# Low parts of the plain gate/up tiles on VectorE, two tiles interleaved in every down pass, and four gate blocks moved into the last prompt heads

## The reference, cut to what matters

```
h = rmsnorm(x, g_mix)
qa, ka, va, cq, ckv, kpe, ga, gb = split(h @ w_in)
oa = sliding-window attention with sinks and a relative bias (8 heads)
ob = latent attention: q from cq @ w_uq, keys and values from ckv @ w_ukv (8 heads)
mixed = sigmoid(ga) * (oa @ w_oa) + sigmoid(gb) * (ob @ w_ob)
x = x + mixed @ w_out
h = rmsnorm(x, g_ffn)
x = x + (silu(h @ w_gate) * (h @ w_up)) @ w_down        # D_FF = 2816
```

## Time and profile before

| what | us |
|---|---|
| median of three runs | 1826.62 (1825.90 to 1828.09) |
| the profiled execution | 1825.76 |
| its span, first to last instruction | 1824.0 |
| PE busy | 1771.6 |
| DVE busy | 1046.9 |
| ACT busy | 704.1 |
| POOL busy | 616.0 |

### The profile page before, as it was taken

The page is one execution under the profiler, slowest core; times in us unless marked ns, Lnnn a source line. Parts: engine busy times, 40 slices in busy tenths (PEclk is TensorE's granted clock), DMA queues, the critical chain, the costliest instruction groups (busy, mean ns, idle before and its releaser), DMA issues.

```text
span 1824.0 us, 31441 instructions
## 1 busy us (share of the span) xinstructions
PE 1771.6 (97%) x12122; PEld 1697.2 (93%) x12122; DVE 1046.9 (57%) x1590; ACT 704.1 (39%) x1401; POOL 616.0 (34%) x345
## 2 busy tenths in 40 slices
PE   7999999999999999999999999999999999999997
PEld 7988887999989999999999888789999999999997
DVE  5564455475773745647546444556758555647464
ACT  5254345313432433324432634443234333334243
POOL 1322321133344444534333233112332443534432
PEclk9999999999999999999999999999999999999999
DMA  5233523342123131321222234143321231321212
GB/s 166 87 113 109 145 76 99 129 166 72 66 75 99 59 104 53 104 86 62 68 92 70 76 124 130 64 136 129 137 77 62 78 104 51 104 81 64 98 53 87
DMA packets 63787, 171.24 MB, mean 94 GB/s; under 512 B 8120, under 2 KB 13912, under 8 KB 63512
## 3 DMA queue, kind: packets, MB, share of 16 engines
q1 hardware_dynamic: 62808, 167.73, 28.1%
q10 hardware_dynamic: 864, 1.97, 0.3%
HBM read 151.03 MB, written 19.43 MB: 93 GB/s over the span
## 4 chain that ended last, share of the span: by engine, by line
PE 84%; DVE 7%; ACT 4%; issue 2%; DMA 1%; POOL 1%; SPq 0%; POOLq 0%; DVEq 0%; ACTq 0%
PE acc L1518 36%; PE acc L1359 12%; PE acc L1599 11%; PE psU L1599 9%; PE psS L1599 3%; PE acc L1464 2%; PE psU L1310 1%; PE psU L1324 1%; DMA w_raw<-in_w 1%; PE acc L1289 1%; PE psU L1339 1%; PE acc L1554 1%; ACT w_hi L767 1%; POOL w_lo L703 1%; DVE four L2039 1%
## 5 line engine op out<-in xcount | busy, mean ns | idle before, releaser
L703 POOL TENSOR_TENSOR w_lo<-w_raw,w_hi 128x1024 fp32r<-128x1024 f32 x102 | 248.3, 2435 | 679.7 <-ACT w_hi L767 679.7
L767 ACT ACTIVATE w_hi<-w_raw 128x1024 fp32r<-128x1024 f32 (+2 forms) x194 | 174.0, 898 | 427.0 <-PE acc L1518 386.3
L711 POOL TENSOR_TENSOR w_lo<-w_raw,w_hi 128x512 fp32r<-128x512 f32 (+2 forms) x92 | 143.0, 1555 | 330.4 <-ACT w_hi L767 330.4
L2333 DVE TENSOR_TENSOR xT<-acc,xT 128x640 f32<-128x640 f32 x88 | 72.6, 825 | 199.4 <-PE acc L1518 197.1
L730 POOL TENSOR_TENSOR s_raw<-w_raw 128x512 f32<-128x512 f32 x72 | 106.2, 1475 | 158.5 <-DVE s_lo L1996 110.4
L1518 PE MATMUL acc<-act_hi,w_hi 128*128 128x320 f32 x654 | 149.9, 310 | 4.9 <-DVE act_lo L2045 4.8
L1518 PE MATMUL acc<-act_lo,w_hi 128*128 128x320 f32 x654 | 148.9, 308 | 0.0
L1518 PE MATMUL acc<-act_hi,w_lo 128*128 128x320 f32 x654 | 148.8, 308 | 0.0
L787 ACT ACTIVATE s_hi<-s_raw 128x512 fp32r<-128x512 f32 x144 | 90.2, 627 | 147.7 <-POOL s_raw L730 55.0
L1359 PE MATMUL acc<-h_hi,w_hi 128*128 128x320 f32 x512 | 139.0, 353 | 1.5 <-DVE gate L1976 1.2
L1996 DVE TENSOR_TENSOR s_lo<-s_raw,s_hi 128x512 fp32r<-128x512 f32 x144 | 112.1, 793 | 47.9 <-ACT s_hi L787 47.2
(11 more groups left out here) (347 smaller groups left out, 4695.8 us busy)
## 6 DMA issues: line engine op xcount, KB each, us to landing
w_raw<-in_w SPq DMA_DIRECT2D x116, 512.0 KB, 3.5
w_raw<-in_w_pairs SPq DMA_DIRECT2D x72, 512.0 KB, 3.4
w_raw<-in_w SPq DMA_DIRECT2D x48, 256.0 KB, 2.6
gates<-gate SPq DMA_DIRECT2D x32, 320.0 KB, 2.2
tmp<-gates SPq DMA_DIRECT2D x32, 320.0 KB, 3.2
w_raw<-in_w SPq DMA_DIRECT2D x32, 320.0 KB, 2.7
cb_t<-in_cb_t SPq DMA_DIRECT2D x16, 256.0 KB, 3.0
cb_v<-in_cb_v SPq DMA_DIRECT2D x16, 256.0 KB, 2.8
```

Source lines behind the costliest of these rows:

```text
L703: pool.tensor_tensor(w_lo[:, s, :], w_raw[:, s, :], w_hi[:, s, :], ALU.subtract).then_inc(s_w_lo, 1)
L711: pool.tensor_tensor(w_lo[:, n % 2, 0:cols], w_raw[:, n % 2, 0:cols], w_hi[:, n % 2, 0:cols], ALU.subtract).then_inc(s_w_lo, 1)
L767: act.activation(w_hi[:, slot, 0:cols], w_raw[:, slot, 0:cols], ACT.Copy).then_inc(s_w_hi, 1)
L2333: then(evac, dve.tensor_tensor(two(xT[:, c, :]), acc2(m), two(xT[:, c, :]), ALU.add), alone=g is None and c == KD - 1)
```

## The change

There are three edits. First, POOL no longer makes the low parts of the lead's units 2 to 7; VectorE does, in a new function `lead_weight`, at six places of `lead_pairs`, where `lead_scale`, `lead_up` and `lead_gate` of later tiles also move ahead of some operands' low parts. ScalarE's order is unchanged. Second, every down pass begins with `two_tiles`; in the first four passes one block of tile 1 (`early`) goes ahead of the last block of tile 0. `w_started` of tile 1 then comes with its second block. Third, the first four blocks of the gate tile `GATE_SB`, of which one stood behind the `turn_b` of each of three pairs of heads and one behind the last pair, go into the last two pairs of heads, two in each.

```diff
--- before.py
+++ after.py
@@ -732,8 +732,6 @@
             for l in range(DEPTH):
                 first = 2 if l == 0 else 0
                 lows(l * UNITS + first, UNIT_FF + 2 - first)
-                for n in range(2, 2 * FF_LEAD):
-                    low(l * UNITS + (UNIT_FF + n))
                 for i in range(PAIRS):
                     sums(l, i)
                     turn = turn_of(i) if i < PAIRS - 1 else len(FF_PASSES) - 1
@@ -1402,9 +1400,11 @@
                         if n:
                             gate_blocks(l, g, range(k, k + n))
                         if e == j:
+                            if j >= J_SB - 4:
+                                gate_blocks(l, GATE_SB, [j - J_SB + 4])
                             turn_b(l, j + 1)
-                    if J_SB - 8 <= j < J_SB - 2:
-                        gate_blocks(l, GATE_SB, [(j - J_SB + 8) // 2])
+                    if j >= J_SB - 4:
+                        gate_blocks(l, GATE_SB, [j - J_SB + 5])
                     pv_heads(l, j)
                     if j + 2 < J_SB:
                         turn_b(l, j + 2)
@@ -1528,19 +1528,15 @@
                 seen = l * (D_FF // P) + sum(FF_PASSES[:p + 1])
                 wait_alone(pe, s_act, seen - 1)
                 whole = p < len(FF_PASSES) - 1 or l < DEPTH - 1
-                if p == len(FF_PASSES) - 1:
-                    two_tiles(l, unit, tile_, FF_PASSES[p], seen)
-                    with pe.Fori(0, KD // 2 - (1 if whole else 2)) as i:
-                        pair(l, i, unit + 2, tile_ + 2, act_hi, act_lo, FF_PASSES[p])
-                else:
-                    with pe.Fori(0, KD // 2) as i:
-                        pair(l, i, unit, tile_, act_hi, act_lo, FF_PASSES[p], (s_act, seen))
+                two_tiles(l, unit, tile_, FF_PASSES[p], seen, 2 if p == len(FF_PASSES) - 1 else 1)
+                with pe.Fori(0, KD // 2 - (1 if whole else 2)) as i:
+                    pair(l, i, unit + 2, tile_ + 2, act_hi, act_lo, FF_PASSES[p])
                 if not whole:
                     last_tiles(l, unit + KD - 2, tile_ + KD - 2, FF_PASSES[p])
 
-            def two_tiles(l, unit, tile_, n_k, seen):
-
-                for s, blocks in ((0, range(n_k - 1)), (1, range(2)), (0, range(n_k - 1, n_k)), (1, range(2, n_k))):
+            def two_tiles(l, unit, tile_, n_k, seen, early):
+
+                for s, blocks in ((0, range(n_k - 1)), (1, range(early)), (0, range(n_k - 1, n_k)), (1, range(early, n_k))):
                     if blocks[0] == 0:
                         unit_ready(l * UNITS + unit + s)
                         tile_free(l * TILES + tile_ + s)
@@ -1553,7 +1549,7 @@
                             for half in range(2):
                                 last = pe.matmul(acc[:, s, half, 0:HALF], w, x[:, k, half * HALF:(half + 1) * HALF],
                                                  start=s0, stop=s1)
-                                if k == 2 * s and w is whi and x is act_hi and half == 0:
+                                if k == early * s and w is whi and x is act_hi and half == 0:
                                     last.then_inc(w_started, 1)
                     if blocks[-1] == n_k - 1:
                         last.then_inc(acc_full, 1)
@@ -1701,8 +1697,6 @@
                 pe.wait_ge(s_spread, l * 16 + 16)
                 pe.wait_ge(s_kcopy, l * (H_B // 2) + H_B // 2)
                 head_jobs(l)
-                gate_blocks(l, GATE_SB, [3])
-
                 pe.wait_ge(heads_loaded, l * 16 + 16)
                 pe.wait_ge(s_o, l * O_GROUPS + O_SB)
                 for r in range(4):
@@ -2090,6 +2084,13 @@
                                   rstd5[:, :].unsqueeze(2).to_broadcast([P, T // P, P]), ALU.mult).then_inc(s_lead_diag, 1)
                 dve.wait_ge(s_lead_copied, l + 1)
 
+            def lead_weight(l, n):
+
+                unit, slot = l * UNITS + UNIT_FF + n, (UNIT_FF + n) % 2
+                dve.wait_ge(s_w_hi, unit + 1)
+                dve.wait_ge(w_started, unit)
+                dve.tensor_tensor(w_lo[:, slot, :], w_raw[:, slot, :], w_hi[:, slot, :], ALU.subtract).then_inc(s_w_lo, 1)
+
             def lead_gate(l, t):
 
                 fill(l, TILE_FF + 2 * t)
@@ -2117,34 +2118,40 @@
             def lead_pairs(l):
 
                 norm(l, 0)
+                lead_weight(l, 2)
                 lead_gate(l, 0)
                 mix_rows(l, 0)
                 norm_low(l, 0)
                 norm(l, 1)
+                lead_weight(l, 3)
                 mixed_low(l, 0)
                 lead_scale(l, 0)
                 lead_up(l, 0)
                 lead_low(l, 0)
+                lead_weight(l, 4)
                 mix_rows(l, 1)
                 norm_low(l, 1)
                 lead_gate(l, 1)
                 norm(l, 2)
+                lead_weight(l, 5)
+                lead_scale(l, 1)
+                lead_up(l, 1)
                 mix_rows(l, 2)
                 mixed_low(l, 1)
                 norm_low(l, 2)
-                lead_scale(l, 1)
-                lead_up(l, 1)
                 lead_low(l, 1)
+                lead_gate(l, 2)
+                lead_weight(l, 6)
                 norm(l, 3)
                 mix_rows(l, 3)
                 mixed_low(l, 2)
-                norm_low(l, 3)
-                lead_gate(l, 2)
-                mixed_low(l, 3)
-                part_low(l, 0, A11)
                 lead_scale(l, 2)
                 lead_up(l, 2)
+                lead_weight(l, 7)
+                norm_low(l, 3)
+                mixed_low(l, 3)
                 lead_low(l, 2)
+                part_low(l, 0, A11)
                 lead_gate(l, 3)
                 lead_scale(l, 3)
                 part_low(l, 0, S2)
```

## The result

The changed kernel took 1811.41 us (median of four runs, 1810.37 to 1813.48), the kernel before 1827.01 beside it (1825.90 to 1828.09): ratio 0.9915, 95% interval [0.9904, 0.9927]. The forecast was 1809.9, within 1804.5 to 1817.5.

The account below looks back on a forecast made before the run. PE, busy 97% of the 1824.0 us span, was taken as the bound. Gains of 7.6 (lead), 6.2 (passes) and 2.9 (heads) sum to 16.7 us off 1825.76, so 1809.1, or 1809.9 as median; range 1804.5 to 1817.5.

Parts of the forecast that it names:

- The lead's 5.6 us: Lead, tile 2 to the pairs' first product: each layer loses 5.6 us, which low parts on VectorE would win.
- about 1.7 us because the granted clock fell: Lead: share of each layer's 5.6 us loss put down to 3.4 us at half clock behind the 2.8 us wait.
- The replay of VectorE's order: Lead: hand-timed VectorE queue; no tile waits for its low part, or tile 7 by a tenth of a us.
- VectorE's stalls behind POOL: Lead: VectorE would lose its stalls of about 2 us a layer while its own work grows by 6.9 us.
- The hand-over's 1.7 us: Lead to pairs: cost of 0.7 us at the second product plus 1.0 at pair 1's first, each layer.
- free: Rival: the hand-over costs nothing because POOL's sums end in time; 3.4 us more won, 1806.5; chance 0.12.
- all given back: Rival: the hand-over gives back all 7.6 us of the lead's gain, leaving 9.1, 1817.5; chance 0.10.
- The passes' 3.1 us a layer: First four down passes: interleaving covers waits for `act_lo`, 0.41 + 3 x 0.9 = 3.1 us a layer.
- the margin of 0.2 at tile 2: Down passes: tile 2's low part takes 2.45 us of the 2.64 available, so no new wait there.
- the slower rival: Down passes: written-out tiles starve TensorE's queue, 4.5 us a pass, 36 in eight, 1845.9; chance 0.03.
- The heads' 1.45 us: Last prompt heads: moved gate blocks fill PE's waits, gaining 1.45 us a layer, bounds 0 and 2.3.
- The rival that the thinned heads let the clock fall: First two pairs of the last heads: idle PE lowers the clock, 1.7 us lost a layer, 1813.3; chance 0.09.

Follow-up runs that it names:

- the two repeats: The changed kernel with all three edits, measured again twice beside the experiments: 1813.86 us, then 1812.34 us.
- heads-only kernel: Only the third edit (gate blocks in the last two pairs of heads) against the kernel before: 1826.13 us, ratio 1.0.
- the passes alone: Only the second edit (two tiles interleaved in every down pass) against the kernel before: 1821.15 us, ratio 0.9956.
- the swap: Changed kernel with pair 1's first operand ahead of pair 0's last on ScalarE and VectorE: 1808.53 us; changed kernel beside it 1812.34.
- the holds: Changed kernel with POOL's first sum of pair 1 held for pair 0's operands: 1810.02 us; with pair 0's fourth sum held too: 1812.45 us.

## Why the prediction was right, point by point

**Sum.** 16.7 us were forecast and 16.2 are there by stage. The median came 1.5 above the forecast; the profiles show two things that can have done it, the run's end, about 1 us longer, and the 3.1 us that some executions lose behind the heads. That the two medians differ by 15.6, so near to 16.7, is in part luck: beside the two repeats the kernel before was at 1826.09 and 1821.36, and the changed kernel 12.2 and 9.0 under it (last section). The lower end of the range comes to 1804.2 by its own terms, not 1804.5; nothing hangs on it.

**The lead's 5.6 us** measured 5.46 a layer, but the split was wrong. I had put "about 1.7 us because the granted clock fell" beside the 2.8 us wait. The heads-only kernel, with the wait and without the fall, was as long. The whole loss was VectorE's order, and what I took for the clock's price was the next wait, which the slow matmuls covered. Had an edit only kept the clock up there, it would have won nothing.

**The replay of VectorE's order** held: PE waits for no tile of the lead, and the low parts of tiles 3 to 7 were ready within 0.2 us of the times put down for them. For tile 7, whose low part I had ready at 516.0 with a tenth to lose (517.44 on this trace's clock, where tile 2 starts 1.44 later), it is ready at 517.57, and the weight load waits 0.15 us for it in either layer, the row `w_lo` L2092 here. Mis-sized was the term of VectorE's stalls behind POOL, about 2 us a layer: the busy time says about 9. It did not enter the replay, which counted every instruction at its unstalled time. Waits of PE's weight loads in the changed kernel, whole run:

```profile
PEld acc L1518 <- POOL w_lo L711: 0.6, 2, 0.3
...
PEld acc L1550 <- DVE act_lo L2039: 0.4, 1, 0.4
PEld acc L1518 <- DVE w_lo L2092: 0.3, 2, 0.2
```

**The hand-over's 1.7 us** measured 1.42 and 1.77, in another division: 0.31 and 0.62 at the second product where I had 0.7 (`s_lo` itself was stretched by 0.5, not 0.7), and 1.55 and 1.64 at pair 1's first, where I had 0.65 + 1.0. Both rivals on it, free and all given back, fell.

**The passes' 3.1 us a layer** measured 3.3 and 2.8 here, 3.08 and 3.07 alone. The rows above show no new wait for POOL's `w_lo`: the margin of 0.2 at tile 2 was enough, and the 0.3 is still the last pass's. Of the waits for `act_lo` one of 0.44 is left, at 1523.13 in layer 1's second pass, where I had put all below 0.15; it is there in every profile with both the new lead and the passes, and not in that of the passes alone. It is most of what layer 1 wins less than layer 0. Code written out ahead of the loops cost nothing that can be seen, which ends the slower rival.

**The heads' 1.45 us** measured 1.15. The two waits of 0.78 and the one of 0.69 went and 0.81 for the last copy came, as the prediction had them. Of the idle times in the first two pairs (1.2 and twice 0.6) only one of 0.60 came. Counted from the same score, the last `pv` starts 0.96 earlier where I had 1.2 (14.79 us instead of 15.75), and the next stage follows it after 1.91 instead of 1.8. PE's timeline after, layer 0:

```profile
284.20 1.09 PE L1322 MATMUL psU<-pT,vB 128*64 128x128 f32 x16 [0.60 <-ACT pT L967]
...
297.79 2.02 PE L1707 MATMUL psS<-qB,w_ukT 64*128 64x128 f32 x16 [0.81 <-ACT o_all L972]
```

The rival that the thinned heads let the clock fall (0.09) was half true: in some executions, in layer 0 alone in the profiles, and at 3.1 us, not 1.7 a layer; a second fall of the clock stood among the prediction's own signs of being wrong. I had looked for the danger in the first two pairs, which lost their blocks; the runs point at the block behind the last pair, which I had priced as cover for a copy only.

## What to carry to other kernels

Before a stretch at low clock is charged for, ask what would have ended next at full clock: behind a wait for an in-order engine the slow matmuls may only fill that engine's time. Where VectorE stands behind POOL, an instruction's place in the queue costs one POOL operation, so put the operand wanted next one place forward rather than hold POOL back: the swap kept 2.4 us, the holds 1.1 at most. And a block of full matmuls between two thin stretches may be worth more than the wait it hides: with one behind the heads the clock fell there in no profile, and no timed run had a low mean clock.

## What was not expected of the hardware

The same instructions met the same 2.8 us wait in the lead of the kernel before and of the heads-only kernel: the clock fell to half for 3.4 us behind it in both layers of the one profile and in neither layer of the other. Behind the heads it fell for 6.8 us in three profiles and not at all in others of the same shape. What tips it stays open.

A run's time goes with its mean granted clock in the changed kernel (1809.10 and 1809.90 at 0.998, 1813.86 to 1815.60 at 0.994), but only loosely in the kernel before: there 42 runs beside the experiments took 1816.09 to 1829.56, and those at 0.996 alone 1818.17 to 1827.35. The kernels with the old lead all spread widely (13.5, 12.5 and 11.0 us for the kernel before, the passes alone and the heads alone), each kernel with the new lead by 1.6 to 6.5. Why is not shown, since none of the shortest executions was profiled. One thing in the old lead is as finely balanced as the hand-over above: in all six layers profiled, `t_lo` began 0.03 us behind POOL's `w_lo` and took 3.06 us where 0.82 is usual. If it began first in some executions, these would lose up to 2.2 us less a layer; that is an estimate, and too small for the whole spread.
